# Low parts of the dense weights over the raw blocks, and four expert blocks loaded among the dense ones

## What is computed

```python
h = rms_norm(x, norm_mix)
(mq, mk, mv, mo, mi, mf, aq, ak, av, gu, gv, gate_pre) = split(h @ w_in, SPLIT_POINTS)   # 8,456 columns
ya = mixer_mlstm(...)              # 4 heads of 128, chunks of 64
yb = mixer_dilated_attention(...)  # 3 groups of 4 heads of 64
yc = mixer_spatial_gating(...)     # 4 groups of 128 channels
g = sigmoid(gate_pre.reshape(b, s, 3, 1024))
merged = g[0] * (ya @ w_branch_a) + g[1] * (yb @ w_branch_b) + g[2] * (yc @ w_branch_c)
x = x + merged @ w_out
x = x + memory_cross_attention(rms_norm(x), rms_norm(mem), w_xq, w_xkv, w_xo)
x = x + grouped_moe(rms_norm(x), router, w_gate, w_up, w_down)   # top 2 of 16 experts, one group of 4
```

## Time and profile before

| | |
|---|---|
| median of 3 runs | 578.33 us (577.7 to 578.63) |
| the profiled execution, span | 576.9 us, granted TensorE clock 0.997 of full speed |
| PE busy | 563.2 us, 98% of the span |
| DVE, ACT, POOL busy | 276.5, 234.9 and 20.8 us |
| moved by DMA | 165.19 MB, mean 286 GB/s |
| chain that ended last | PE 90%, DVE 3%, ACT 2%, DMA 1% |

### The profile page before, as it was taken

How to read it: one execution, slowest core, us unless ns; L and a number is a source line. 1 busy time by engine, 2 the same in 40 slices (tenths; PEclk the granted TensorE clock), 3 DMA queues, 4 the chain that set the end, 5 groups by cost and what they waited for, 6 DMA issues and landing times.

```text
span 576.9 us, 7293 instructions
## 1 busy us (share of the span) xinstructions
PE 563.2 (98%) x2875; PEld 379.4 (66%) x2875; DVE 276.5 (48%) x415; ACT 234.9 (41%) x314; POOL 20.8 (4%) x15
## 2 busy tenths in 40 slices
PE   8999999999998999999999999999999999999995
PEld 7889888888876778888888786434444434443333
DVE  4463686976588653997765627311222221220002
ACT  6664673584594555833655643211111111111112
POOL 0000000050010000000100120000000000000000
PEclk9999999999999999999999999999999999999998
DMA  8994674566633338656656798999999999999962
GB/s 306 406 302 151 217 258 147 196 252 208 219 110 110 110 103 310 240 157 213 198 167 198 282 427 348 351 425 425 426 428 425 427 425 426 427 425 427 425 282 75
DMA packets 46300, 165.19 MB, mean 286 GB/s; under 512 B 4276, under 2 KB 5432, under 8 KB 33720
## 3 DMA queue, kind: packets, MB, share of 16 engines
q1 hardware_dynamic: 43872, 159.12, 71.8%
q10 hardware_dynamic: 2392, 5.59, 2.8%
HBM read 163.63 MB, written 1.06 MB: 285 GB/s over the span
## 4 chain that ended last, share of the span: by engine, by line
PE 90%; DVE 3%; ACT 2%; DMA 1%; DVEq 1%; issue 1%; POOL 0%; SPq 0%
PE ps L2010 19%; PE ps L1562 15%; PE ps L1554 15%; PE ps L1555 15%; PE ps L2029 10%; PE ps L1535 5%; PE ps L2054 3%; PE ps L1926 3%; DMA w_raw<-in_w_in 1%; PE ps L1729 1%; PE ps L1703 1%; PE ps L1840 1%; PE ps L1863 1%; PE ps L1917 1%; PE ps L1617 1%
## 5 line engine op out<-in xcount | busy, mean ns | idle before, releaser
L969 DVE TENSOR_TENSOR w_lo<-w_raw,w_hi 128x2048 fp32r<-128x2048 f32 (+2 forms) x52 | 113.9, 2208 | 58.9 <-ACT w_hi L565 58.3
L1554 PE MATMUL ps<-w_hi,act_hi 128*128 128x512 f32 (+1 forms) x288 | 112.2, 392 | 0.0
L1555 PE MATMUL ps<-w_hi,act_lo 128*128 128x512 f32 (+1 forms) x288 | 110.1, 384 | 0.0
L565 ACT ACTIVATE w_hi<-w_raw 128x2048 fp32r<-128x2048 f32 (+2 forms) x52 | 95.3, 1852 | 30.3 <-PE ps L1562 25.2
L2010 PE MATMUL ps<-e_raw,xg 128*64 128x512 f32 x400 | 89.1, 596 | 0.0
L1562 PE MATMUL ps<-w_lo,act_hi 128*128 128x512 f32 (+1 forms) x288 | 70.3, 386 | 0.0
L2010 PEld LDWEIGHTS ps<-e_raw,xg 128*64 128x64 f32 x400 | 27.4, 137 | 53.4 <-issue 53.2
L1554 PEld LDWEIGHTS ps<-w_hi,act_hi 128*128 128x128 f32 x288 | 54.1, 188 | 10.9 <-issue 0.7
L1555 PEld LDWEIGHTS ps<-w_hi,act_lo 128*128 128x128 f32 x288 | 54.1, 188 | 10.0
L1562 PEld LDWEIGHTS ps<-w_lo,act_hi 128*128 128x128 f32 x288 | 52.6, 188 | 10.9 <-issue 0.7
L884 ACT ACTIVATE gu<-ps,rs_slot 128x512 f32<-128x512 f32 x16 | 11.0, 687 | 96.2 <-PE ps L2010 96.2
(11 more groups left out here) (292 smaller groups left out, 710.6 us busy)
## 6 DMA issues: line engine op xcount, KB each, us to landing
w_raw<-in_w_in SPq DMA_DIRECT2D x30, 1024.0 KB, 5.2
e_raw<-in_w_expert_gate SPq DMA_DIRECT2D x25, 1024.0 KB, 15.1
e_raw<-in_w_expert_up SPq DMA_DIRECT2D x25, 1024.0 KB, 18.0
e_raw<-in_w_expert_down SPq DMA_DIRECT2D x22, 1024.0 KB, 20.9
w_raw<-in_w_expert_down SPq DMA_DIRECT2D x10, 1024.0 KB, 22.5
w_raw<-in_w_expert_gate SPq DMA_DIRECT2D x7, 1024.0 KB, 13.2
w_raw<-in_w_expert_up SPq DMA_DIRECT2D x7, 1024.0 KB, 16.2
w_raw<-in_w_xkv SPq DMA_DIRECT2D x4, 1024.0 KB, 5.1
```

The source lines that it names most:

```text
L565: A(bview(w_hi, b, blocks[b].shape), bview(w_raw, b, blocks[b].shape), ACT.Copy).then_inc(hi_done, 1)
L969: V.tensor_tensor(bview(w_lo, b, sh), bview(w_raw, b, sh), f32(bview(w_hi, b, sh)), ALU.subtract).then_inc(lo_done, 1)
L1554: MM(o, xh[:, t0 + k, i * P:(i + 1) * P], wh[:, k], start=first and k == 0, stop=False)
L1555: MM(o, xl[:, t0 + k, i * P:(i + 1) * P], wh[:, k], start=False, stop=False)
```

## The change

1. `w_lo` is no longer a ring of its own: it has the address of `w_raw`. DVE writes the low part of a block over the raw block.
2. Since PE reads the low part from the raw slot, `weight_block(b)` now waits for `mm_done` of block b-4, and no longer for its split.
3. The 32 KB per partition that are freed hold `e_early`, four buffers for expert blocks 0 to 3. They are loaded right behind dense blocks 10, 11, 12 and 13 in SP's list, without a wait of their own. Their landings are counted on four semaphores that had been used once at the start.
4. The buffers of expert blocks 9, 11, 13 and 15 move with `w_lo`. Expert blocks from 4 on keep their waits and their place in the list; the loop starts at 4.

```diff
+EARLY = range(10, 14)
...
+        w_raw_at = place["at"]
         w_raw = sb("w_raw", [P, RING, BLK])
         w_hi_at = place["at"]
         w_hi = sb("w_hi", [P, RING, BLK], f32r)
-        w_lo_at = place["at"]
-        w_lo = sb("w_lo", [P, RING, BLK], f32r)
+        w_lo = at("w_lo", w_raw_at, [P, RING, BLK], f32r)
+        e_early = sb("e_early", [P, RING, BLK])
...
-        e_raw = [None] * RING + [at("e_raw_4", ...), ...]
-        e_raw += [at(f"e_raw_{8 + 2 * i + k}", (w_hi_at, w_lo_at)[k] + 4 * BLK * i0, [P, BLK])
+        e_raw = [e_early[:, k, :] for k in range(RING)] + [at("e_raw_4", ...), ...]
+        e_raw += [at(f"e_raw_{8 + 2 * i + k}", (w_hi_at, w_raw_at)[k] + 4 * BLK * i0, [P, BLK])
...
+        EARLY_LANDED = {"first_half_landed": 16, "second_half_landed": 16, "x_pair_landed": 16, "x": 32}
+        e_in_slot[0:RING] = [s[n] for n in list(EARLY_LANDED)[:3]] + [sT["x"]]
...
                 if b >= RING:
-                    sp.wait_ge(hi_done, split_count(b - RING))
-                    sp.wait_ge(lo_done, split_count(b - RING))
+                    sp.wait_ge(mm_done, b - RING + 1)
                 sp.dma_start(bview(w_raw, b, blocks[b].shape), blocks[b]).then_inc(w_in_slot[b % RING], 16)
...
-            for b in range(8, NB1):
-                weight_block(b)
...
-            for n in range(NB2):
+            for b in range(8, NB1):
+                weight_block(b)
+                if b in EARLY:
+                    expert_load(b - EARLY[0])
+
+            for n in range(RING, NB2):
...
-                elif n == 4:
+                else:
                     sp.wait_ge(s_sq["x1"], 1)
-                else:
-                    sp.wait_ge(hi_done, split_count(NB1 - RING + n))
-                    sp.wait_ge(lo_done, split_count(NB1 - RING + n))
                 expert_load(n)
```

More of the change, by code:

```diff
@@ L157, in build_program @@
         m_at = region(POST + 8192)
-        assert not any(v % LINE for v in (w_hi_at, w_lo_at, act_at, q_at, zq_at, zo_at, zqk_at, zv_at, zg_at, tg_at, m_at))
+        assert not any(v % LINE for v in (w_hi_at, w_raw_at, act_at, q_at, zq_at, zo_at, zqk_at, zv_at, zg_at, tg_at, m_at))
         zif_at = region(NT * 8 * 4)
@@ L266, in build_program @@
         assert place["at"] <= m_at + POST, (place["at"], m_at)
-        e_raw = [None] * RING + [at("e_raw_4", q_at, [P, BLK]), at("e_raw_5", m_at + POST, [P, BLK]), e_raw_6, e_raw_7]
-        e_raw += [at(f"e_raw_{8 + 2 * i + k}", (w_hi_at, w_lo_at)[k] + 4 * BLK * i0, [P, BLK])
+        e_raw = [e_early[:, k, :] for k in range(RING)] + [at("e_raw_4", q_at, [P, BLK]), at("e_raw_5", m_at + POST, [P, BLK]), e_raw_6, e_raw_7]
+        e_raw += [at(f"e_raw_{8 + 2 * i + k}", (w_hi_at, w_raw_at)[k] + 4 * BLK * i0, [P, BLK])
                   for i, i0 in enumerate(W_HI_ORDER) for k in range(2)]
@@ L441, in e_slot @@
             turns = n // ring + 1 + (len(range(k, NB2, E_FIRST)) if later else 0)
[L442 to L446, removed]
+            earlier = list(EARLY_LANDED.values()) + [0] * (8 - RING) + list(LOADED.values())
+            before_ = earlier[k] if k < len(earlier) else 0
+            return e_raw[k], e_in_slot[k], before_ + 16 * turns
         SCATTERS = 2 * NE + 3
```

## The result

| | before | after |
|---|---|---|
| median of the runs | 578.47 us (577.7 to 578.63, 4 runs) | 597.79 us (594.9 to 598.79, 4 runs) |
| ratio, with its 95% interval | | 1.0328 [1.0302, 1.0354] |
| profiled execution, span | 576.9 us | 593.1 us |
| its granted TensorE clock | 0.997 | 0.994 |

The kernel is 19.3 us slower in the median and 16.2 us slower between the two profiled spans. The forecast was 593.0 with a range of 584.5 to 600.0.

The account below looks back on a forecast made before the run. The prediction took PE to bound the kernel; six stalls of 1.2, 2.9, 2.3, 3.7, 1.0 and 3.6 us, together 14.7, added to 578.33 gave 593.0 us, with an 8-in-10 range of 584.5 to 600.

Parts of the forecast that it names:

- What bounds the kernel: Whole kernel: PE busy 563.2 of 576.9 us; in the expert part PE, not the loads, sets the pace.
- The low part in the raw slot: DVE's subtraction written over the raw block: same operands and shape, costed at 0.
- The landings: Dense loads, issue to landing: 5.2 us (`w_in`), 4.9 (`w_out`, also taken for `w_xo`), 4.4 (768 KB).
- Place 2: Block 33, behind block 29: late high part delays `attn_exp(4)` and the `pT` copy PE needs, 2.9 us.
- place 3: Block 36, behind block 32: late high part and copy against PE's turns at 218.00, 2.3 us.
- Place 5: Block 48, behind block 44: 5.0 us late, delaying DVE's `residual_add` before PE's turns, 1.0 us.
- Place 1: Block 11, behind block 7: late high part delays `move(4)` and the `pre` copies before PE's turns of `zif`, 1.2 us.
- the queue of SP: Expert blocks 0 to 3 behind dense blocks 10 to 13: cost 0, at most one transfer, 2.5 us.
- Place 4: Block 38, behind block 34: load beside 2 MB on ACT's queue, high part 7.0 late, `branch(C_A)` 6.2 late, 3.7 us.
- Place 6: Block 53, behind block 49: late low part delays DVE's scaling of `xq`, then PE's logits and the softmax, 3.6 us.
- The expert loads that go from the end of the dense part: Later expert blocks land up to 4 x 2.5 us earlier; PE does not wait for them, gain 0.
- Near misses: Other late blocks with margins under 1 us: costed at 0; four of them falling would be up to 4 us.

Follow-up runs that it names:

- raw5: The changed kernel with five raw slots instead of four and three early expert blocks, dense loads waiting for PE's end of block b-5: 578.48 us, ratio 1.0001.
- wait_only: The kernel before with one edit, a dense load waits for PE's end of block b-4 and no longer for its split: 596.65 us, ratio 1.0312.
- late_experts: The changed kernel with expert blocks 0 to 3 loaded behind block 53 instead of among blocks 10 to 13: 597.04 us, ratio 1.0323.
- three_places_before: The kernel before, without the change, with the splits of 53 and 11 moved back and residual_add put before the low part of 48: 586.88 us, ratio 1.0152.

## Why the prediction was right

The mechanism, the six places and the size are those predicted. The sum is nearer to the truth than its terms, whose errors partly cancel. By its steps:

- **What bounds the kernel.** PE, in both parts. The shift is constant over the expert part. Right.
- **The low part in the raw slot, 0.** `raw5` shows it.
- **The landings.** The 5.2 us of `w_in` was the median of loads of which many are issued in pairs, some 2.2 us apart. Issued alone, block 33 took 4.76 us and block 11, in `wait_only`, 4.89. Place 2 came out at 2.57 us for 2.9 and place 3 at 2.23 for 2.3. Place 5 was 0.93 for 1.0.
- **Place 1** was sized at 1.2 and measured 1.54; `wait_only` and `late_experts` measured 0.85. The step that failed is the sentence that gives the queue of SP a cost of 0: it took an expert block's transfer for over when PE's next end allows the next dense load, a block's time later. The first expert block, issued right behind block 10, landed 8.12 us after its issue, 3.1 us behind the issue of block 11. The two misses, a landing taken 0.3 too dear and a transfer taken at nothing, nearly cancelled.
- **Place 4** was sized at 3.7 and measured 4.77. That `branch(C_A)` sets the sum is right: PE waits at 38, 39 and 40, and each wait takes part of the same delay, of which the last decides. But `branch(C_A)` was 7.1 us late and not 6.2 (261.07 against 247.43, less the 6.54 lost before). Its high part was 7.3 late for 7.0. And the gap of 0.82 was hardly taken up, for the prediction left out that block 39's own load is late too (8.53 us): it held back ACT, and ACT's high part of block 40 held back DVE.

```profile
246.46 1.91 ACT L563 ACTIVATE w_hi<-w_raw 128x2048 fp32r<-128x2048 f32 x1 [0.89 <-DMA w_raw<-in_w_branch_a]
252.29 2.29 DVE L967 TENSOR_TENSOR w_lo<-w_raw,w_hi 128x2048 fp32r<-128x2048 f32 x1 [0.59 <-ACT w_hi L563]
261.07 1.27 DVE L1212 SCALAR_TENSOR_TENSOR tg<-tg,ps 128x512 f32<-128x512 f32 x2
```

- **Place 6** came out at 3.90 for 3.6. `xq` ended 4.0 us late (332.75 against 316.35, less the 12.40 lost before), as the load took 5.54 us for 4.9. Of the two paths that the prediction names, the one over the logits is not the one: before the change PE came to the turns of `xq` only 1.03 us after DVE had finished it, so it idled 2.88 us there, about 1 less than the delay. The softmax behind it carries the whole delay, and PE waits again for DVE at its end (`xkv`, DVE's last step there). The first row is of the kernel before, the second of the kernel after:

```profile
317.38 1.04 PE L1535 MATMUL ps<-ident,xq 128*128 128x128 f32 x8
```

```profile
345.29 3.07 PE L1838 MATMUL ps<-xpT,xkv 128*128 128x256 f32 x13 [0.56 <-DVE xkv L1307]
```

- **The expert loads that go from the end of the dense part.** The prediction let all later blocks land up to four transfers earlier. With PE's shift taken off, blocks 4 and 5 landed about 8 us earlier and the others, from 6 on, not at all. It had no effect, since PE waits for none of them.
- **Near misses** were costed at 0 and were 0.18 (block 50). **Stalls add**: right, the sum of the steps is the shift at the end.
- **The Trainium skill's rule for the landing**, SBUF — State Buffer, section "The DMA setup-cost knee", gave an estimate of 4.4 us for 1 MiB and 589 for the sum. The landings were mostly 4.7 to 5.2 us where nothing else was under way (medians 4.9 and 5.0), and never under 4.7; the trace doesn't agree with the rule, and the rows were the better guide.
- **The term that was missing** is the granted clock. The sum gave 14.7, the profiled execution lost 16.4 on PE, and the medians differ by 19.3. The first difference, 1.7, is the sizes above. The second, 2.9, is not in this trace, whose run (594.9 us) is the fastest of the four. All four runs of the kernel after are longer than the forecast. How far the clock explains this is the last section.

The range ended at 600 for other reasons (block 38 at its bound, near misses). That it held is luck: these were of the size of the missing term.

## What to carry to other kernels

When a ring's slot is shared by a load and by what is made from it, the question isn't whether the compute engine has cover, but what stands behind the preparing step in each in-order list; price the landing there, place by place. One slot more than the depth of the preparation gives the load back its lead and made the whole loss vanish here. Before moving a step back, look at both lists for what it stands before at its new place, and at every queue whose waits count that step, SP's included: one wait there made every later landing 14 us late, and with a lead that had shrunk to 5.3 us it cost 8.5 us in the median, two hundred microseconds later. When the DMA engines are full and PE is busy, measure the lead from landing to use and whether it shrinks. The early loads were no gain here, since they took nothing off the stretch where the engines are full.

## What the runs showed of the hardware

After a stall PE may come back at half of its clock. Stretches of the kernel after around PE's idle time of 2.88 us, which ends at 332.81 (columns as above; the clock is the third number from the right):

```profile
332.00:334.00 2.00, 1.19 (x8) 1.11 (x8) 0.88 (x3) 1.21 (x2) 0.00 (x0) 0.84 0.01 4
334.00:336.00 2.00, 1.75 (x6) 1.20 (x5) 1.27 (x2) 1.05 (x2) 0.57 (x1) 0.50 0.22 24
336.00:338.00 2.00, 2.00 (x9) 1.72 (x8) 0.82 (x3) 0.00 (x0) 1.06 (x1) 0.81 0.14 17
338.00:340.00 2.00, 2.00 (x11) 1.72 (x10) 1.77 (x7) 1.93 (x7) 0.00 (x0) 1.00 0.00 0
```

The granted clock is 0.50, that is 1.2 GHz instead of 2.4, from about 333.4 to 336.8 us, and PE was busy most of that time: at most 1.7 us, half of 3.4. Here it cost nothing in the end, for PE still waited 0.56 us for DVE before 345.29. It isn't the same from run to run. The kernel after has one such stretch in its profile; in `wait_only` there are four, after the stalls at blocks 30, 33, 38 and 51. Those in the attention make the 3.2 us by which its steps at 30 to 34 are larger (8.0 against 4.8), 1.6 us each. The PEclk line of `wait_only` (a short stretch shows only as an 8, and not at all where it falls on the border of two slices):

```profile
PEclk9999999999999898989999899999999999999998
```

The kernel before and `raw5`, without these stalls, have none until the end. The four runs of the kernel after, by clock, are 594.9 us at 0.994, 597.07 at 0.988, 598.5 at 0.987 and 598.79 at 0.984. The two ends are 3.9 us apart at 0.010 of clock. The profiled one is the run at 594.9, and its one stretch cost nothing, so no part of its 16.4 us over the kernel before is seen to be the clock. The clock can then explain the 2.9 us from there to the median of 597.79, which would be two stretches of 1.6 us, as an estimate. Of the 4.6 us between the sum and the median that is the larger part; the other 1.7 are the sizes of the places. The three slower runs have no trace, so this rests on their granted clock and on `wait_only`. What decides whether a stall is followed by such a stretch is open: stalls of 2 to 3 us at the same place were followed by one in some runs and by none in others. No kernel was made to settle it.

A load can stand still behind another engine's queue. Block 38's load was issued by SP 1.7 us after ACT had issued the last of 2 MB, and had its first packet 3.85 us after its issue, when ACT's queue was nearly done. The DMA engines were full all that time (share 1.01).

With the DMA engines full, 1 MB blocks landed about 2.5 us apart (77 intervals from 368.2 to 559.2 us in the kernel before, and from 383.0 to 573.3 in `three_places_before`), whether PE waited for them or not.
